# Opening of a two-block model on one core: sums of squares, attention heads in pairs, output projection by banks, expert mask

## What is computed

```python
h = rmsnorm(x, g_mix)                                   # mean of squares over 1024 channels
z = einsum('bsd,de->bse', h, w_in)                      # 2048 columns: 512 pooled, 3 x 512 q, k, v
a_out = pool_mixer(z[..., :512], w_pool, pool_scale)
b_out = dilated_attention(q, k, v, rel_bias)            # 8 heads of 64, scores masked and biased
x = x + einsum('bse,ed->bsd', concatenate([a_out, b_out]), w_out)
h = rmsnorm(x, g_ffn)
logits = h @ w_router + b_router                        # 32 experts
topv, topi = lax.top_k(logits, 4); gates = softmax(topv)
# every token goes through its 4 experts; rank = place of the token among those of its expert
x = x + moe(...)                                        # gate and up 1024x2048, down 1024x1024 per expert
```

## Time and profile before

| | |
|---|---|
| median of three runs | 2718.29 us (2712.18 to 2718.5) |
| profiled execution | 2707.69 us, span 2705.6 us |
| TensorE busy | 2224.5 us, 82% of the span |
| DVE, ACT busy | 1376.0 us (51%), 605.9 us (22%) |
| chain that ended last | PE 44%, DMA 36%, DVE 14%, ACT 4% |
| DMA | 1054.64 MB, mean 390 GB/s |

### The profile page before, as it was taken

One profiled execution on the slowest core, in us unless ns is written; L12 is line 12 of the kernel. 1 busy time (PEld: TensorE's weight loads), 2 busy tenths in 40 slices (PEclk: granted clock), 3 DMA queues, 4 the chain that ended last, 5 costly groups with the idle time before them and its releaser, 6 DMA issues.

```text
span 2705.6 us, 34585 instructions
## 1 busy us (share of the span) xinstructions
PE 2224.5 (82%) x12777; PEld 1059.6 (39%) x12777; DVE 1376.0 (51%) x3811; ACT 605.9 (22%) x1468; POOL 492.9 (18%) x534
## 2 busy tenths in 40 slices
PE   9899999999999999997865579678578588575566
PEld 6744444444444444995431123225123235121112
DVE  2412221222221222667677777784676875587754
ACT  0300110101000111232222242332232442232212
POOL 1000000000000000003333333332323332233340
PEclk9989999999999999998987889788799889687779
DMA  7679999999999997559999999999999999999994
GB/s 253 265 322 409 429 428 429 428 429 428 429 429 428 429 428 334 184 214 390 420 419 421 421 419 419 420 419 417 420 418 417 409 389 417 419 408 421 421 420 174
DMA packets 134696, 1054.64 MB, mean 390 GB/s; under 512 B 15633, under 2 KB 16057, under 8 KB 44465
## 3 DMA queue, kind: packets, MB, share of 16 engines
q0 software_dynamic: 75104, 540.07, 48.3%
q1 hardware_dynamic: 59472, 513.03, 45.9%
HBM read 1051.97 MB, written 2.63 MB: 390 GB/s over the span
## 4 chain that ended last, share of the span: by engine, by line
PE 44%; DMA 36%; DVE 14%; ACT 4%; issue 2%; POOL 0%; SPq 0%; DVEq 0%; POOLq 0%; ACTq 0%
DMA big<-in_uv,small 23%; PE ps L793 16%; DMA big<-in_w_gate_up 11%; PE ps L1267 6%; DVE big L2239 5%; PE ps L783 5%; PE ps L947 4%; PE ps L1074 1%; DMA ring<-in_uv,small 1%; PE ps L829 1%; PE ps L1060 1%; PE ps L643 1%; PE ps L1025 1%; PE ps L715 1%; PE ps L811 1%
## 5 line engine op out<-in xcount | busy, mean ns | idle before, releaser
L1267 PE MATMUL ps<-big,small 64*64 64x512 f32 x3840 | 612.0, 749 | 409.8 <-ACT small L1725 409.5
L2425 POOL DMA_INDIRECT big<-in_uv,small x480 | 452.3, 942 | 2059.3 <-DVE small L2219 1164.4
L793 PE MATMUL ps<-big 128*64 128x512 f32 x3072 | 701.2, 600 | 10.4 <-DMA big<-in_w_gate_up 6.7
L2239 DVE SCALAR_TENSOR_TENSOR big<-big,ps 128x1024 f32<-128x1024 f32 x480 | 576.2, 1217 | 261.5 <-DMA big<-in_uv,small 261.3
L1267 PEld LDWEIGHTS ps<-big,small 64*64 64x64 f32 x3840 | 151.6, 158 | 786.7 <-ACT small L1725 581.7
L793 PEld LDWEIGHTS ps<-big 128*64 128x64 f32 x3072 | 205.6, 137 | 395.8 <-issue 357.9
L1969 DVE COPY big<-ps 128x512 f32<-128x512 f32 x32 | 22.1, 692 | 417.0 <-PE ps L793 417.0
L1725 ACT ACTIVATE small<-small 128x64 f32<-128x64 f32 x512 | 150.2, 340 | 326.2 <-DVE small L2268 273.5
L1719 ACT ACTIVATE small<-small 128x2 f32<-128x2 f32 x224 | 51.5, 230 | 580.1 <-DVE big L2239 542.1
L1955 DVE TENSOR_TENSOR big<-ps,big 128x256 f32<-128x256 f32 x64 | 27.2, 424 | 283.4 <-PE ps L811 283.4
L947 PEld LDWEIGHTS ps<-hT,ring 128*128 128x128 f32 x1152 | 134.5, 196 | 23.9 <-issue 20.3
(11 more groups left out here) (352 smaller groups left out, 2120.5 us busy)
## 6 DMA issues: line engine op xcount, KB each, us to landing
big<-in_w_gate_up SPq DMA_DIRECT2D x128, 2048.0 KB, 20.7
big<-in_w_down SPq DMA_DIRECT2D x64, 2048.0 KB, 22.3
ring<-in_peer_w_q SPq DMA_DIRECT2D x48, 512.0 KB, 12.8
ring<-in_ple_w_gate SPq DMA_DIRECT2D x22, 512.0 KB, 11.2
ring<-in_w_in SPq DMA_DIRECT2D x16, 512.0 KB, 8.0
ring<-in_a_w_in SPq DMA_DIRECT2D x16, 512.0 KB, 4.8
ring<-in_b_w_q SPq DMA_DIRECT2D x16, 512.0 KB, 13.1
ring<-in_b_w_o SPq DMA_DIRECT2D x16, 512.0 KB, 14.5
```

What stands on the lines that cost most here:

```text
L793: last = pe.matmul(ps[side * CAP:(side + 1) * CAP, bank + b, :], o, w[:, at:at + BANK], start=start, stop=stop, skip_group_check=True)
L1267: last = pe.matmul(ps[tokens_ if by_halves else at, bank, :], diagonal(k)[tokens_, :], rows(k)[tokens_, D + z * BANK:D + (z + 1) * BANK], ...
L2239: ins = dve.scalar_tensor_tensor(r, r, 1.0, tok, op0=ALU.mult, op1=ALU.mult, accum_out=dots[:, k % PICKS:k % PICKS + 1])
L2425: pool.indirect_dma_start(out=rows(k), out_offset=None, in_=io[f"uv{n // UNITS}"], in_offset=bass.IndirectOffsetOnAxis(ap=rows_at[:, at:at ...
```

## The change

It has four parts. (1) The sums of squares: DVE adds the four pairs of squared chunks into one (`sum_squares` on DVE), so that in the first norm two matmuls with ones remain; in the second norm four matmuls whose moving operand is a single column of ones give the sums with tokens on partitions, so that the root needs no transpose. (2) Attention in pairs: the scores of both heads of a chunk are issued in turn, on the two row halves of the array, and their values in turn on the two column halves; one copy takes both. `prob` has four buffers. All of chunk 0 of the projection stands behind the first scores, then half a chunk behind each transpose. (3) The last three chunks of the output projection are multiplied bank by bank (`finish_bank`); DVE adds, scales, and sums each bank by itself, and the router's first three chunks stand before bank 3. (4) The mask is found by replacing the four largest logits by a small number and comparing; both tiles go through each step side by side. Indices, comparisons and the count follow after `select(0)`, in `routed_gates`, and the two matmuls of the count come last and go to bank 4.

```diff
-        prob = [hT[:, k * SPAN:(k + 1) * SPAN] for k in range(2)]
+        prob = [(hT, winsum)[k // 2][:, k % 2 * SPAN:(k % 2 + 1) * SPAN] for k in range(4)]
...
-            def sum_squares(k):
-
-                for j in range(4):
-                    pe.wait_ge(sq_ready, 4 * k + j + 1)
-                    for c in (2 * j, 2 * j + 1):
-                        last = pe.matmul(ps[:, 7, 0:T], ones, tile(mT, c), start=(c == 0), stop=(c == DT - 1))
-                last.then_inc(ss_done, 1)
+            def sum_squares():
+
+                pe.wait_ge(sq_ready, 5)
+                pe.matmul(ps[:, 7, 0:T], ones, tile(mT, 0), start=True, stop=False)
+                pe.matmul(ps[:, 7, 0:T], ones, tile(mT, 1), start=False, stop=True).then_inc(ss_done, 1)
...
-            def scores(h):
-                lo = 64 * (h % 2)
-                q, k = tile(q1, h // 2), tile(k1, h // 2)
-                if h == 0:
+            def scores(p):
+                q, k = tile(q1, p), tile(k1, p)
+                if p == 0:
                     pe.wait_ge(S["qk_ready"], 2)
                     pe.wait_ge(S["u_copied"], 6)
-                if h >= 2:
-                    pe.wait_ge(S["prob_ready"], h - 1)
-                pe.matmul(ps[:, 4 + h % 2, 0:P], q[lo:lo + DH, 0:P], k[lo:lo + DH, 0:P], start=True, stop=True)
-                pe.matmul(ps[:, 4 + h % 2, P:SPAN], q[lo:lo + DH, P:T], k[lo:lo + DH, 0:T], start=True, stop=True)\
-                    .then_inc(S["score_done"], 1)
+                else:
+                    pe.wait_ge(S["biased"], 2 * p)
+                for i, lo in enumerate((0, DH)):
+                    pe.matmul(ps[:, 4 + i, 0:P], q[lo:lo + DH, 0:P], k[lo:lo + DH, 0:P], start=True, stop=True)
+                for i, lo in enumerate((0, DH)):
+                    pe.matmul(ps[:, 4 + i, P:SPAN], q[lo:lo + DH, P:T], k[lo:lo + DH, 0:T], start=True, stop=True)\
+                        .then_inc(S["score_done"], 1)
...
+            def values(p):
+                pe.wait_ge(S["pt_ready"], 2 * p + 2)
+                if p:
+                    pe.wait_ge(S["mix_ready"], 4 + p)
+                for i in range(3):
+                    for lo, pt in zip((0, DH), probT):
+                        at = (i // 2) * BANK + 2 * p * DH + lo
+                        last = pe.matmul(ps[lo:lo + DH, 7, min(i, 1) * P:(min(i, 1) + 1) * P], v1[:, at:at + DH],
+                                         pt[:, i * P:(i + 1) * P], start=(i < 2), stop=(i != 1), skip_group_check=True)
+                last.then_inc(S["pv_done"], 1)
...
             scores(0)
+            out_blocks(0, range(DT))
             scores(1)
-            for h in range(HEADS1):
-                out_blocks(h // 2, (range(0, 4), range(4, DT))[h % 2])
-                turn(h)
-                if h + 2 < HEADS1:
-                    scores(h + 2)
-                if h >= 1:
-                    values(h - 1)
-            out_blocks(4, range(DT))
-            values(HEADS1 - 1)
-            for c in range(5, DT):
-                out_blocks(c, range(DT))
...
+            for p in range(HEADS1 // 2):
+                for i in range(2):
+                    turn(2 * p + i)
+                    out_blocks(p + 1, (range(0, 4), range(4, DT))[i])
+                values(p)
+                if p + 2 < HEADS1 // 2:
+                    scores(p + 2)
+            def finish_bank(b):
+
+                for c in range(5, DT):
+                    pe.wait_ge(S["mix_ready"], 4 + (c - 4) + 1)
+                    w = chunk(first["w_out"] + c)
+                    for e in (2 * b, 2 * b + 1):
+                        last = pe.matmul(half(0, e), w[:, e * P:(e + 1) * P], msrc(c), start=False, stop=(c == DT - 1),
+                                         skip_group_check=True)
+                    if b == 3:
+                        last.then_inc(w_used, 1)
+                    elif c == DT - 1:
+                        last.then_inc(S["score_done"], 1)
...
+            for b in range(3):
+                finish_bank(b)
+            route(range(0, 3))
+            finish_bank(3)
+            route(range(3, DT)).then_inc(w_used, 1)
+            pe.wait_ge(sq_ready, 10)
             for tt in range(TT):
-                last = pe.transpose(ps[:, 5, tt * P:(tt + 1) * P], rs[:, tt * P:(tt + 1) * P], ident)
-            last.then_inc(S["root_turned"], 1)
+                for i in range(2):
+                    at = i * T + tt * P
+                    last = pe.matmul(ps[:, 7, tt:tt + 1], rs[:, at:at + P], ones[:, 0:1], start=(tt == 0 and i == 0),
+                                     stop=(i == 1), skip_group_check=True)
+            last.then_inc(ss_done, 1)
             for tt in range(TT):
                 for c in range(DT):
                     last = pe.transpose(ps[:, 2 * tt + c // 4, (c % 4) * P:(c % 4 + 1) * P],
...
-            def copy_o(h):
-                lo = 64 * (h % 2)
-                act.wait_ge(S["pv_done"], h + 1)
-                act.copy(tile(mT, 4 + h // 2)[lo:lo + DH, :], ps[lo:lo + DH, 7, 0:T])\
-                    .then_inc(S["mix_ready"], 1)
+            def copy_o(p):
+                act.wait_ge(S["pv_done"], p + 1)
+                act.copy(tile(mT, 4 + p), ps[:, 7, 0:T]).then_inc(S["mix_ready"], 1)
...
+            def sum_squares(j, to, src, at):
+
+                dve.wait_ge(sq_ready, at + j + 1)
+                ins = dve.tensor_tensor(to, to if j > 1 else tile(src, 0, 512), tile(src, j, 512), ALU.add)
+                if j < 3:
+                    link(ins)
+                else:
+                    ins.then_inc(sq_ready, 1)
+
+            for j in range(1, 4):
+                sum_squares(j, tile(mT, 0, 512), mT, 0)
             dve.memset(upad, 0.0).then_inc(dve_step, 1)
...
-            add_to_x("w_out", 8)
...
+            for b in range(4):
+                if b < 3:
+                    dve.wait_ge(S["score_done"], HEADS1 + b + 1)
+                else:
+                    used_through(dve, "w_out", 8)
+                dve.tensor_tensor(tile(xT, b, 512), ps[:, b, :], tile(xT, b, 512), ALU.add).then_inc(x_ready, 1)
+                dve.wait_ge(x_ready, b + 1)
+                for c in (2 * b, 2 * b + 1):
+                    dve.tensor_scalar(tile(hT, c), tile(xT, c), col("g_ffn", c), None, ALU.mult)\
+                        .then_inc(S["u_ready"], 1)
+                if b:
+                    sum_squares(b, rs[:, :], sq1, 5)
+            dve.memset(r_four, 3e38).then_inc(dve_step, 1)
+            step.n += 1
...
+            for tt in range(TT):
+                step.wait(step.n - 1)
+                mark(dve.match_replace(left(tt), four(tt), lg(tt), -3e38))
+            for tt in range(TT):
+                step.wait(step.n - 1 + tt)
+                dve.tensor_tensor(r_mask[:, tt * 32:(tt + 1) * 32], lg(tt), left(tt), ALU.is_gt).then_inc(S["mask_ready"], 1)
+            for tt in range(TT):
...
             def routed_gates():
+                dve.wait_ge(S["rank_done"], 2)
+                link(dve.tensor_reduce(r_cntf, ps[0:1, 4, 64:96], AX_X, ALU.max))
+                dve.tensor_copy(r_cnt, r_cntf).then_inc(S["count_ready"], 1)
+                for tt in range(TT):
+                    idx = r_idx[:, tt * 8:tt * 8 + 8].bitcast(U32)
+                    link(dve.max_index(idx, top(tt), lg(tt)))
+                    link(dve.tensor_copy(r_idxf[:, tt * 4:tt * 4 + 4], idx[:, 0:TOP_K]))
+                    for k in range(TOP_K):
+                        mark(dve.tensor_scalar(r_hot[:, tt * 128 + k * 32:tt * 128 + (k + 1) * 32], i32c,
+                                               r_idxf[:, tt * 4 + k:tt * 4 + k + 1], None, ALU.is_equal))
+                    step.wait()
...
```

More of the change, by code:

```diff
@@ L728, in _, with route @@
             scores(0)
+            out_blocks(0, range(DT))
             scores(1)
-            for h in range(HEADS1):
-                out_blocks(h // 2, (range(0, 4), range(4, DT))[h % 2])
-                turn(h)
-                if h + 2 < HEADS1:
-                    scores(h + 2)
-                if h >= 1:
-                    values(h - 1)
-            out_blocks(4, range(DT))
-            values(HEADS1 - 1)
-            for c in range(5, DT):
-                out_blocks(c, range(DT))
-            w = chunk(first["w_router"])
-            for j in range(4):
-                pe.wait_ge(sq_ready, 4 + j + 1)
-                for c in (2 * j, 2 * j + 1):
-                    last = pe.matmul(ps[:, 7, 0:T], ones, tile(mT, c), start=(c == 0), stop=(c == DT - 1))
-                if j == 3:
-                    last.then_inc(ss_done, 1)
-                for c in (2 * j, 2 * j + 1):
+            for p in range(HEADS1 // 2):
[16 more added lines that the diff above has]
+                        last.then_inc(S["score_done"], 1)
+            def route(cs):
+                w = chunk(first["w_router"])
+                for c in cs:
                     pe.wait_ge(S["u_ready"], DT + c + 1)
@@ L1856, in _ @@
                     normalised(s - 1)
```

(16 more changed lines are left out.)

99 lines of the change are left out of this document (37 added, 62 removed).

## The result

| | before | after |
|---|---|---|
| device time, median of 4 runs each, one chip | 2715.30 us (2712.18 to 2718.50) | 2688.04 us (2686.99 to 2689.50) |
| profiled execution, and its span | 2707.69, 2705.6 | 2688.48, 2686.3 |
| first gather starts | 133.47 | 116.43 |

The medians are 27 us apart (0.9900 of before). The two profiled executions are 19.2 us apart (spans 19.3), where the prediction had 18.8. The 8 us between the two readings belong to the runs of before on that chip; experiments 1 and 2 repeat the comparison.

A forecast was written before the change was run, and what follows sets the result against it. TensorE bounds the expert stage at first, the weight stream at its end. Terms of 17.85 us to the first gather and 0.9 for the clock total 18.8: 2688.9 from 2707.69, or 2699 from the median 2718.29; range 2688 to 2710.

The forecast's parts named there:

- Theory A: Whole kernel: the gain is what the opening saves up to the first gather, some 17 us, passed on by later stages.
- First norm: Sums of squares in the opening norm: two matmuls remain of eight, VectorE's adds are hidden; minus 2.6 us.
- Attention and projection: From line 725 to the last projection matmul: heads in pairs take 40.3 us instead of 47.4; minus 7.1 us.
- the step that was doubted: Softmax chain in attention: odd head's probabilities ready 2.4 us behind scores; rival that it paces, shared chance 0.14.
- Behind the projection: From the projection's end through sums and root: bank-by-bank work leaves 4.55 us of 9.6; minus 5.1 us.
- Mask: Expert selection in routing: paired small operations take 2.0 us instead of 4.3; minus 2.25 us.
- Ranks and count: Between mask and first gather: VectorE waits for three matmuls, not five, and the count leaves the path; minus 0.8 us.
- Clock: TensorE's granted clock around the first gather: falls again, costing 4.8 us instead of 5.7; minus 0.9 us.
- the likely case: Around the first gather the clock falls again, costing 3 to 6 us; total 2695 to 2703, chance 0.60.
- the first rival: Around the first gather the clock stays at 2.4 GHz; all 5.7 us return, gain 23.6, total 2694.7, chance 0.16.
- the router's weights: Rival at the router: weights land late, near 103.2 us, wanted at 104.6; at most 1.4 us gainable ahead; shared chance 0.14.
- the clock stayed at 1.00 in attention: Answers the slower rival: clock falls in attention and stays at 1.2 GHz, plus 19 us, 2737; chance 0.04.

The follow-up runs named there:

- experiment 1: The kernel before itself again, no edit, on a second chip: 2711.06 us, ratio to before 1.0004.
- experiment 2: The changed kernel (after) again, no edit, on the second chip: 2690.30 us, ratio to before 0.9930.
- experiment 11: The changed kernel (after) a third time, no edit, on the chip of experiments 10 and 12: 2689.23 us, ratio to before 0.9920.
- Experiments 10 and 12: After with five 256-column filler matmuls, two behind the ranks, three in the first gather; 10 also widens router and sums to 128 columns: 2687.24 us; 12 fillers alone: 2686.16.
- experiment 3: After with router and sum matmuls widened to 128 columns and one 256-column matmul behind the ranks: 2690.56 us, ratio to before 0.9920.
- experiment 4: After with attention in single heads again (order, copies and two buffers too), the other three parts kept: 2697.85 us, ratio to before 0.9962.
- 7: After with each pair's scores and values issued one head after the other instead of in turn: 2690.62 us, one run.
- experiment 8: After with the projection's last three chunks multiplied whole again, VectorE's adds waiting for the last and the router behind: 2693.2 us, one run.
- experiment 6: Before with 256-column filler matmuls: five ahead of the ranks, two behind them, three in the first gather: 2708.67 us, ratio to before 1.0001.

## Why the prediction was right

The time was 2688.04, for 2699.0 forecast with 2688 to 2710. It lies inside the range by 0.04 us, which is luck, and outside the 2695 to 2703 that were given 0.60. What held is the gain. Against before on the same chip the gain is 19.5 us (experiment 2) and 21 (experiment 11), for 18.8. The distance from 2699 comes from the median that it was taken from, 2718.29, some 8 us above those of later chips and 10.6 above the profiled execution; from that execution the prediction had 2688.9, for 2688.48. Theory A holds: before to after, expert 0 starts 17.0 us earlier, the last expert's last matmuls 17.7, and the span ends 19.3 earlier. The last 1.6 are within the spread of the third column above. So that 18.8 and 19.3 agree within 0.5 is in part chance: up to the second gather, where the terms of the prediction end, this pair of executions is 16.6 us apart, and 2.7 come behind it.

Term by term, to the first gather (17.85 forecast, 17.04 measured; counted from the first norm's matmuls, 17.7 in after and 18.5 in experiments 2 and 11):

- *First norm, 2.6.* 3.45 became 0.86: 2.6. In this pair of executions 0.6 of it is hidden by a start that was 0.36 later and by chunk 0, 8.85 for 8.59.
- *Attention and projection, 7.1.* 47.4 became 39.7 (40.96 less the router's 1.26): 7.7. The values took 0.81 for 0.9, the scores 0.86 for 1.05; both are what the prediction had as perfect overlap (0.80 and 0.85). What sets the period is the step that was doubted: from the scores' end (79.93) to the odd head's transposes (82.19) it is 2.26 us of VectorE's chain, for 2.4 forecast, and the period is 6.21 for 6.5. The prediction's sum per pair is misadded: its terms give 6.27, not 6.1; the 6.5 that it went on with is 6.27 and the wait.
- *Behind the projection, 5.1.* 3.80 us and the router's 1.26, for 3.35 and 1.2: 4.6 gained. The size was off in one place. The router's last 20 records last 2.32 us and the sums stand behind them; I had put them beside the add. The one-column group took 0.97, for 0.85.
- *Mask, 2.25.* 1.42 us for 2.0: 2.85 gained. Steps in pairs hid more than I took.
- *Ranks and count, 0.8.* Nothing in this execution (mask to gather 2.76 us), since the mask waited 0.6 us for transposes at the low clock and the ranks ran at it too. In experiment 2, where they were not held up, mask to gather takes 1.95 us (114.63 to 116.58) for 2.65: 0.7.
- *Clock, 0.9.* It fell again, as forecast. The cost is gather 7.08 for 3.72, 40 records at 11.56 for 8.80 and 0.8 ahead of the gather (2.76 for 1.95), 6.9 in this execution, and 4.6 in experiments 2 and 11, where 4.8 was taken. Before loses 5.7 in the same way. So the term was right in the likely case (1.0) and of the wrong sign here (1.2 more than before, 0.8 of them already in the line above). The price of the first rival, 4.8 us, is not settled. Experiments 10 and 12 are 2.0 and 3.1 us below after, and their fillers cost 1.4 themselves (1.1 in the gather, 4.8 for 3.7, and 0.3 ahead of it), so a clock that stays up for nothing would give 3.4 to 4.5 by the times. By the landmarks it would give 2.2 to 3.0: the 2.0 of the gather, and the 0.2 to 1.0 that is not lost again of the 2.6 in expert 0's matmuls.

The step against the first rival was that thin work brings the clock down without a long pause. It held: the clock fell in all six profiles without fillers that have no long pause there (after and experiments 2, 3, 4, 7 and 11), in after and in 4 with TensorE busy all the time. What it is in that work that decides was not taken apart. The Trainium skill (TensorE: Matmul & The Clock Gate, Part 1) ties the low level to idle time; in after the clock fell between 112 and 114 us with TensorE busy 2.00 of 2.00, so here the row decides and not that rule. The other rivals: the router's weights were not waited for (line 757 follows line 744 without a gap at 104.52); the clock stayed at 1.00 in attention, from 69 to 96 us, with TensorE busy 26.67 of 27.00.

## What to carry to other kernels

Where a stage behind is paced by a stream whose buffers are released by use, look at what comes ahead of the first use: here a gain inside it was mostly lost again (1.6 to 2.4 of 2.6 us, by the means). Work that uses half the array is cheap in pairs (scores 0.86 us for two heads, 0.85 for one): put two halves side by side first, and in turn if it costs nothing. Let the last accumulation finish bank by bank, so that the vector work lies under matmuls (6 us in experiment 8). If the clock falls in a stretch of thin matmuls, a few wide ones among them are worth a trial: here they kept it at 1.00 in four profiles of four, and gave 2 to 3 us in after and 1 in before, neither clear of the noise. And before believing a gain to the microsecond, run the kernel before again on another chip, since here its median moved by 5.6 us (2715.3 to 2709.7) and that of after by 2.3 at most.

## What the runs showed of the hardware that was not expected

- TensorE's clock fell while it was busy all the time, as far as a profile shows it in which the ends of matmuls are modelled. It did so twice: in after between 112 and 114 us, among the transposes behind the one-column group, and in experiment 4 between 118 and 120 us, at the same place. In experiment 4 it came back between 122 and 124 us, on the last transposes and matmuls of 32 columns, and fell once more in the gather (windows, columns as in the earlier trace rows):

```profile
118.00:120.00 2.00, 2.00 (x17) 1.97 (x17) 0.63 (x2) 1.33 (x2) 0.00 (x0) 0.87 0.95 344
120.00:122.00 2.00, 2.00 (x11) 2.00 (x10) 1.68 (x15) 0.39 (x2) 0.00 (x0) 0.50 0.87 309
122.00:124.00 2.00, 2.00 (x17) 2.00 (x15) 0.19 (x1) 1.77 (x4) 0.00 (x0) 0.78 0.10 39
```

- In before the clock fell once more after 193.5 us. TensorE had a pause of 0.60 us, then ran 16 records that contract over 32 rows only, from 189.6 to 193.3 us, at 1.00. The low window stands behind them and holds matmuls of the experts over all 128 rows, with TensorE busy 3.50 of 3.50. The cause is open.

```profile
193.50:197.00 3.50, 3.50 (x11) 1.07 (x8) 0.00 (x0) 0.00 (x0) 0.00 (x0) 0.53 1.00 417
```

- A group of eight records with one moving column takes 0.97 us, and with 128 columns 1.01 (experiment 3). The weight loads of that group are busy 0.97 us as well, so it is these 128x128 loads, not the columns, that seem to set the pace.
- The first 32 records of a kernel do not always run at one pace. They took 8.59 us in before, 8.85 in after, 9.43 in experiment 1 and 10.18 in experiment 6, at a granted clock of 1.00. The first of them are the slow ones: experiment 6 has 6 records in each 2 us from 8 to 12 us, and 11 from 14 us on, which is nearly the factor of two between the clock's two levels, though the column shows 1.00. With the landing of the first load this moves the first norm's matmuls by up to 2.3 us from one execution to another (15.06 in before, 17.39 in experiment 11). The cause is open.
